# PEER gates added to a cleared table by 512 indirect transfers, expert rows added in memory, and expert blocks reordered

## Chip, cores and metric

The kernel runs on one core of a Trainium2 chip. The time is the device time of one execution in microseconds (us), the median of three runs.

## What is computed

Two transformer blocks on 512 tokens of width 1024, all in float32. The first has a spatial gating branch, a neighbourhood attention and a mixture of experts: 64 experts with 256 hidden units, of which each token takes 8. The second has a latent attention (MLA, 8 heads), a retention branch and a PEER layer with 16384 experts of one hidden unit each. The two parts that the change touches are, cut to what matters:

```
# experts (moe_ffn)
scores = sigmoid(h @ w_router); idx = top_k(scores + b_router, 8)
wts = scores[idx] / sum(scores[idx]) * 2.5
routed[tok] += swiglu(h[tok], w_gate[e], w_up[e], w_down[e]) * wt      # for each of a token's 8 experts
out = swiglu(h, w_sh_gate, w_sh_up, w_sh_down) + routed                # the shared expert
# PEER: 8 heads; a head's key scores against two sets of 128 keys
# 16 best of each set, 16 best of their 256 sums -> 16 of 16384 experts and softmax gates
y[tok] = sum over heads and their 16 experts of  gate * gelu(h[tok] . u[expert]) * v[expert]
```

## The kernel before

Each float32 operand of a large product is split into a high and a low half (`w_hi` by ScalarE, `w_lo` = raw - high by VectorE), and a product is three matmuls: high by high, high by low, low by high. Stages follow one another as blocks: when an `nc.Block()` ends, all engines wait for each other, which the trace shows as waits for `PEq`. `load` (L1125) is such a block: SP issues loads and waits for them.

**Experts (L1211).** Tokens stand in blocks of 128 rows: 4 blocks for the shared expert (`b < T`, T = 4), then 95: 64 for the experts' first 128 tokens each, 31 for what is over. Their order is two of the first kind, one of the second. Routing (VectorE, with small TensorE products) makes lists of rows for each block (`vtab`, and `tok` = `vtab` / 8). For a block GpSimd gathers the tokens' rows by an indirect transfer (`take`, L1355, four blocks ahead), gathers weights for the over blocks (L1366), and scatters the result (`put`, L1378) to `expert_rows`, which has one row for each of the 4096 pairs of token and slot. SP loads the weights of a base block, 3 MB in three units. TensorE goes `gate_up(b+1)` (24 matmuls), `turn_hidden(b)` (2 transposes), `turn_x(b+3)` (8), `down(b)` (12 matmuls). Between them ScalarE does SiLU and `hidden_high`, VectorE `multiply` and `hidden_low`; both also split the weights. After the last block follows the combine (L1736 to L1791): VectorE makes the slot weights, loads 8 rows and the shared row for each token, and adds them with one multiply-add for each slot.

**MLA attention (L539, called at L1934).** `attend` begins with `load` of a table `spread` of 0.2 KB and then goes through 32 units of 128 queries and a head.

**PEER (L2147).** 64 activation steps `n`, each with two groups of 128 experts: SP loads 1 MB of `peer_u` (two buffers), ScalarE and VectorE split it, TensorE does 48 matmuls, ScalarE applies GELU, SP stores the activations to `acts`. Then 64 value steps, each with 1 MB of `peer_v`, activations and gates fetched back and multiplied, and 48 matmuls. The routing rides on the first steps: in steps 0 to 15 two key products each and VectorE's 16-best searches (`key_round`), in steps 16 to 23 `pick` finds expert numbers, `divide` the softmax. In steps 25 to 57 the gates are put into place by one-hot products: for 4 tokens at a time (128 batches) VectorE makes `hot1` and `hot2`, TensorE multiplies them (`place`, L2523), ScalarE copies the result (`gate_copy`, L2319), and SP stores it to `gates` in 8 pieces of 4 MB. `fetch(0)` and `fetch(1)` (L2261, L2262) follow in step 62.

## Time and profile before

| what | us |
|---|---|
| median of 3 runs (4597.18 to 4601.25) | 4598.52 |
| profiled execution | 4600.06 |
| its span, first to last instruction | 4598.2 |
| TensorE matmul busy (85%) | 3897.8 |
| VectorE busy (54%) | 2492.4 |
| ScalarE busy (37%) | 1722.5 |
| GpSimd busy (10%) | 437.9 |
| mean granted TensorE clock | 0.906 of full |

PE is TensorE, PEld its weight loads, DVE VectorE, ACT ScalarE, POOL GpSimd, SP the queue that issues most transfers. Times inside the trace count from the first instruction. Shares are averages over stages that have different limits, so the stages are read one by one.

### The profile page before, as it was taken

To read this page: it belongs to the slowest core of one execution; us is meant where nothing else is said; L and a number is where in the kernel's file an instruction comes from. 1 tells how busy PE (TensorE), PEld (TensorE's weight loads), DVE (VectorE), ACT (ScalarE), POOL (GpSimd) and SP (SyncE) were. 2 spreads that over 40 slices of the span, in tenths; PEclk is the share of its full clock that TensorE was granted. 3 is DMA by queue.
4 is the path that set the end of the run, shared out by engine and by line. 5 is a ranking of instruction groups with operands and counts; after the bars stand their busy time and mean duration, and the time that the engine had idled before them with its cause. 6 is when DMAs were issued, how large, how long until landed. Compare 5 with 4: busy or idle time off the path is not lost. (4 is left out here: it accounts for less than half of the span.)

```text
span 4598.2 us, 46686 instructions
## 1 busy us (share of the span) xinstructions
PE 3897.8 (85%) x18351; PEld 3144.6 (68%) x18351; DVE 2492.4 (54%) x3841; ACT 1722.5 (37%) x2079; POOL 437.9 (10%) x295
## 2 busy tenths in 40 slices
PE   8677889669999999944399559789999999999999
PEld 1565767557777777733366447678888887888887
DVE  0334513458888888865643433359956663444444
ACT  0222512227777777732122023223233332222222
POOL 0001000014444444410000000000000000000000
PEclk9785879879999999976659779899999999999999
DMA  7210112326666666661002012224445555555554
GB/s 248 80 72 1 38 48 78 145 90 239 245 245 231 228 247 230 233 237 62 21 3 74 9 60 92 73 79 138 138 154 181 181 182 187 198 187 201 186 198 174
DMA packets 250053, 656.69 MB, mean 143 GB/s; under 512 B 44951, under 2 KB 144027, under 8 KB 206316
## 3 DMA queue, kind: packets, MB, share of 16 engines
q1 hardware_dynamic: 208508, 614.78, 37.9%
q0 software_dynamic: 41328, 38.93, 2.5%
q8 instruction: 147, 2.41, 0.2%
q14 instruction: 70, 0.57, 0.0%
HBM read 688.66 MB, written 125.31 MB: 177 GB/s over the span
## 5 line engine op out<-in xcount | busy, mean ns | idle before, releaser
L1503 DVE TENSOR_TENSOR w_lo<-w_raw,w_hi 128x2048 fp32r<-128x2048 f32 x288 | 651.6, 2290 | 172.4 <-ACT w_hi L1413 171.2
L1413 ACT ACTIVATE w_hi<-w_raw 128x2048 fp32r<-128x2048 f32 x288 | 539.3, 1907 | 7.2 <-DMA w_raw<-in_e_w,over_rows 4.3
L2362 DVE TENSOR_TENSOR w_lo<-w_raw,w_hi 128x2048 fp32r<-128x2048 f32 x128 | 293.2, 2290 | 351.1 <-ACT w_hi L2299 350.5
L2299 ACT ACTIVATE w_hi<-w_raw 128x2048 fp32r<-128x2048 f32 x128 | 245.3, 1916 | 523.0 <-DMA w_raw<-in_peer_u 274.9
L1144 PE MATMUL ps_peer<-peer_xT_hi,w_hi 128*128 128x512 f32 x1024 | 408.7, 399 | 4.1 <-DVE w_lo L2362 4.0
L1144 PE MATMUL ps_peer<-w_hi,coef_hi 128*128 128x512 f32 x1024 | 399.6, 390 | 6.1 <-DVE coef_lo L2459 6.1
L1146 PE MATMUL ps_peer<-peer_xT_hi,w_lo 128*128 128x512 f32 x1024 | 399.8, 390 | 0.0
L1145 PE MATMUL ps_peer<-peer_xT_lo,w_hi 128*128 128x512 f32 x1024 | 399.7, 390 | 0.0
L1145 PE MATMUL ps_peer<-w_lo,coef_hi 128*128 128x512 f32 x1024 | 399.3, 390 | 0.0
L1146 PE MATMUL ps_peer<-w_hi,coef_lo 128*128 128x512 f32 x1024 | 399.2, 390 | 0.0
L1626 PE MATMUL ps_gu<-w_hi,h2T_hi 128*128 128x512 f32 x792 | 311.0, 393 | 0.7 <-DVE w_lo L1503 0.7
L1628 PE MATMUL ps_gu<-w_hi,h2T_lo 128*128 128x512 f32 x792 | 310.7, 392 | 0.0
L1627 PE MATMUL ps_gu<-w_lo,h2T_hi 128*128 128x512 f32 x792 | 310.1, 391 | 0.0
L479 DVE TENSOR_TENSOR w_lo<-w,w_hi 128x1024 fp32r<-128x1024 f32 (+5 forms) x116 | 170.0, 1473 | 257.8 <-ACT w_hi L465 257.4
L465 ACT ACTIVATE w_hi<-w 128x1024 fp32r<-128x1024 f32 (+5 forms) x116 | 145.0, 1257 | 352.7 <-DMA w<-in_w_in 231.5
L1626 PE MATMUL ps_d<-w_hi,hidden_hi 128*128 128x512 f32 x396 | 169.3, 428 | 89.7 <-DVE hidden_lo L1515 89.7
L1144 PEld LDWEIGHTS ps_peer<-w_hi,coef_hi 128*128 128x128 f32 x1024 | 192.8, 188 | 47.2 <-issue 7.0
L1144 PEld LDWEIGHTS ps_peer<-peer_xT_hi,w_hi 128*128 128x128 f32 x1024 | 193.3, 189 | 43.4 <-DVE w_lo L2362 5.6
L1146 PEld LDWEIGHTS ps_peer<-peer_xT_hi,w_lo 128*128 128x128 f32 x1024 | 192.7, 188 | 40.7
L1146 PEld LDWEIGHTS ps_peer<-w_hi,coef_lo 128*128 128x128 f32 x1024 | 192.8, 188 | 40.2
L1145 PEld LDWEIGHTS ps_peer<-w_lo,coef_hi 128*128 128x128 f32 x1024 | 192.8, 188 | 39.8
L1145 PEld LDWEIGHTS ps_peer<-peer_xT_lo,w_hi 128*128 128x128 f32 x1024 | 193.1, 189 | 37.9
(475 smaller groups left out, 7584.6 us busy)
## 6 DMA issues: line engine op xcount, KB each, us to landing
w_raw<-in_e_w SPq DMA_DIRECT2D x195, 1024.0 KB, 4.8
w_raw<-in_peer_u SPq DMA_DIRECT2D x64, 1024.0 KB, 5.9
w_raw<-in_peer_v SPq DMA_DIRECT2D x64, 1024.0 KB, 4.8
acts<-act_out SPq DMA_DIRECT2D x64, 512.0 KB, 6.6
gates<-gate_tile SPq DMA_DIRECT2D x8, 4096.0 KB, 15.3
act_back<-acts SPq DMA_DIRECT2D x64, 512.0 KB, 5.8
gates_back<-gates SPq DMA_DIRECT2D x64, 512.0 KB, 7.0
w<-in_w_in SPq DMA_DIRECT2D x26, 1024.0 KB, 7.4
```

Source lines behind the costliest of these rows:

```text
L465: nc.scalar.activation(half_of(w_hi, b, half), half_of(w, b, half), ACT.Copy).then_inc(w_hi_done.sem, 1)
L479: nc.vector.tensor_tensor(half_of(w_lo, b, half), half_of(w, b, half), half_of(w_hi, b, half).bitcast(F32), ALU.subtract) \
L1144: nc.tensor.matmul(out, w_hi, x_hi, start=first, stop=False)
L1145: nc.tensor.matmul(out, w_hi, x_lo, start=False, stop=False)
L1146: return nc.tensor.matmul(out, w_lo, x_hi, start=False, stop=last)
L1413: nc.scalar.activation(w_hi[:, slot(n), :], w_raw[:, slot(n), :], ACT.Copy).then_inc(hi_done.sem, 1)
L1503: nc.vector.tensor_tensor(w_lo[:, slot(n), :], w_raw[:, slot(n), :], w_hi[:, slot(n), :].bitcast(F32), ALU.subtract).then_inc(lo_done.sem, 1)
L1626: nc.tensor.matmul(out, s_hi, m_hi, start=first, stop=False)
L1627: nc.tensor.matmul(out, s_hi, m_lo, start=False, stop=False)
L1628: return nc.tensor.matmul(out, s_lo, m_hi, start=False, stop=last)
L2299: nc.scalar.activation(w_hi[:, n % 2, :], w[:, n % 2, :], ACT.Copy).then_inc(w_hi_done.sem, 1)
L2362: nc.vector.tensor_tensor(w_lo[:, n % 2, :], w[:, n % 2, :], w_hi[:, n % 2, :].bitcast(F32), ALU.subtract) \
```

## The change

Three things change.

1. *PEER gates.* The table `gates` is one column of 128 * 128 * 512 floats. It is cleared by 16 transfers of 2 MB from a zeroed tile, issued ahead of the MLA attention. The one-hot products, their copies and stores go. VectorE makes for each gate its place in the table, and GpSimd adds the gates by indirect transfers with an add, each for 128 tokens and one of 8 * 16 gates: 4 * 128 = 512 transfers. The routing is done for tokens 0 to 255 (8 key steps, 4 pick steps) and then for 256 to 511, so that the first can be added early.
2. *Expert rows.* `put` adds a block's rows to the token's row in memory (`expert_rows` has 512 rows, which the shared expert writes first), each after the landing of the one before. The slot weights are made in the routing, kept in memory, gathered for each block, and applied by ScalarE's copy of the result. The combine reads 4 tiles.
3. *Order in the expert blocks.* `turn_hidden(b)` goes ahead of `gate_up(b+1)`, `hidden_high` and `hidden_low` ahead of the weight halves.

The diff, cut:

```diff
 # experts
@@ sync
+            sp.wait_ge(route_dve.sem, step["wk"])
+            sp.dma_start(scratch["slot_weights"].rearrange("(t p k) o -> p t (k o)", p=P, k=TOPK), wk[:]) \
+                .then_inc(wk_kept.sem, 16)
@@ gpsimd, take(b)
+                nc.gpsimd.indirect_dma_start(
+                    out=wslot[:, r:r + 1], out_offset=None, in_=scratch["slot_weights"],
+                    in_offset=bass.IndirectOffsetOnAxis(ap=vtab[:, r:r + 1], axis=0), bounds_check=V_PAD - 1,
                     oob_is_err=False).then_inc(x_in[b % 4].sem, 16)
@@ gpsimd, put(b)
+                if b == T:
+                    pool.wait_ge(stored[0].sem, 32)
+                    pool.wait_ge(stored[1].sem, 32)
+                else:
+                    pool.wait_ge(stored[(b - 1) % NO].sem, 16 * ((b - 1) // NO + 1))
                 nc.gpsimd.indirect_dma_start(
-                    out=scratch["expert_rows"], out_offset=bass.IndirectOffsetOnAxis(ap=vtab[:, r:r + 1], axis=0),
-                    in_=ob[:, b % NO, :], in_offset=None, bounds_check=V_PAD - 1, oob_is_err=False) \
+                    out=scratch["expert_rows"], out_offset=bass.IndirectOffsetOnAxis(ap=tok[:, r:r + 1], axis=0),
+                    in_=ob[:, b % NO, :], in_offset=None, bounds_check=S - 1, oob_is_err=False, compute_op=ALU.add) \
                     .then_inc(stored[b % NO].sem, 16)
@@ scalar, out(b)
-                    nc.scalar.activation(ob[:, b % NO, h * S:(h + 1) * S], ps_d[:, h, :], ACT.Copy) \
+                    weight = 1.0 if b < T else wslot[:, at_row[b - T]:at_row[b - T] + 1]
+                    nc.scalar.activation(ob[:, b % NO, h * S:(h + 1) * S], ps_d[:, h, :], ACT.Copy, scale=weight) \
@@ scalar, loop over b (vector's loop alike: hidden_low(b) ahead of low(n))
+                hidden_high(b)
                 if b > T:
                     out(b - 1)
...
-                hidden_high(b)
@@ vector, after multiply(0)
+            link(nc.vector.tensor_tensor(sc[:], sc[:], mask[:], ALU.mult))
...
+                ins = nc.vector.tensor_reduce(wk[:, t, :], pick[:, 1], AX, ALU.add)
@@ tensor, loop over b
+                turn_hidden(b)
                 if b + 1 < NB:
                     gate_up(b + 1)
-                turn_hidden(b)
@@ combine
+            sp.dma_start(gate_row[:], scratch["gate_row"][0].partition_broadcast(P)).then_inc(rows_in.sem, 16)
+            for t in range(T):
+                sp.dma_start(rows[:, t, :], scratch["expert_rows"][t * P:(t + 1) * P, :]).then_inc(rows_in.sem, 16)
+            sp.dma_start(x[:], scratch["x_kept"].rearrange("(t p) d -> p t d", p=P)).then_inc(x_back.sem, 16)
...
+                link(nc.vector.tensor_tensor(rows[:, t, :], rows[:, t, :], gate_row[:], ALU.mult))
...
+                nc.vector.tensor_tensor(x[:, t, :], x[:, t, :], rows[:, t, :], ALU.add)
-                for k in range(TOPK):
-                    link(nc.vector.scalar_tensor_tensor(acc, rows[:, t % 2, k, :], wk[:, t, k:k + 1], acc, ALU.mult,
-                                                        ALU.add))
 # second_mixer, between load(causal) and attend
+    zero = core.sb("zero_gates", [P, ZERO // P])
+    zero_gates(core, zero, scratch["gates"])
+def zero_gates(core, zero, gates):
+    with nc.Block() as block:
+        def _(dve):
+            nc.vector.memset(zero[:], 0.0).then_inc(cleared.sem, 1)
+        def _(sp):
+            sp.wait_ge(cleared.sem, 1)
+            for i in range(P * PNK * S // ZERO):
+                sp.dma_start(gates[i * ZERO:(i + 1) * ZERO, :].rearrange("(p n) o -> p (n o)", p=P), zero[:]) \
+                    .then_inc(zeroed.sem, 16)
 # after attend, a block in which SP waits for gates_zeroed
 # peer
-KEY_STEPS = 16
-PICK_STEPS = 2 * T
+KEY_STEPS = PH
+PICK_STEPS = 4
+def route_step(n):
+    pair, at = divmod(n, ROUTE_STEPS)
...
+    return "pick", (2 * pair + t, j)
@@ gpsimd (new)
+            for pair in range(T // 2):
+                for h in range(PH):
+                    for t in (2 * pair, 2 * pair + 1):
+                        if h == 0:
+                            pool.wait_ge(chosen_done.sem, t + 1)
+                        else:
+                            pool.wait_ge(scattered[t].sem, 16 * PK * h)
+                        for k in range(PK):
+                            nc.gpsimd.indirect_dma_start(
+                                out=scratch["gates"],
+                                out_offset=bass.IndirectOffsetOnAxis(ap=where[:, t, h, k:k + 1], axis=0),
+                                in_=chosen[:, 2, t, h, k:k + 1], in_offset=None, bounds_check=P * PNK * S - 1,
+                                oob_is_err=False, compute_op=ALU.add).then_inc(scattered[t].sem, 16)
@@ sync, step NG - 2, ahead of fetch(0)
+                    for t in range(T):
+                        sp.wait_ge(scattered[t].sem, 16 * PH * PK)
@@ vector, divide(t)
+                link(nc.vector.scalar_tensor_tensor(wheref[:], chosen[:, 0, t], float(PNK), chosen[:, 1, t], ALU.mult,
+                                                    ALU.add))
+                nc.vector.tensor_scalar(where[:, t], wheref[:], float(S), at_token[:, t:t + 1], ALU.mult, ALU.add)
@@ vector, tensor, scalar: hots(b), place(b), gate_copy(b), the 12 transposes of chosen go
-                nc.vector.tensor_tensor(hot1[:, q], iota[:].unsqueeze(1).to_broadcast([P, GB, PNK]),
-                    last = nc.tensor.matmul(bank[:, i], hot1[:, q, i], hot2[:, q, i], start=True, stop=True)
```

## Rows read from the trace of the kernel before

**Rows 1.** Busy time by stretch of PEER steps: length, PE, PEld, DVE, ACT, POOL; clock, DMA share.

```profile
3060.00:3180.00 120.00, 120.00 (x530) 99.38 (x530) 115.92 (x513) 35.05 (x50) 0.00 (x0) 1.00 0.41 131
...
3894.00:4598.00 704.00, 699.11 (x3072) 578.12 (x3072) 300.38 (x199) 187.44 (x126) 0.00 (x0) 0.99 0.55 189
```

**Rows 2.** Waits in the expert blocks, 1040 to 2010 us (total, times, longest).

```profile
PE ps_d L1626 <- DVE hidden_lo L1515: 78.3, 94, 2.2
```

**Rows 3.** Timeline of TensorE in one expert block (start us, us).

```profile
1450.37 0.50 PE L1626 MATMUL ps_d<-w_hi,hidden_hi 128*128 128x512 f32 x1 [0.81 <-DVE hidden_lo L1515]
```

**Rows 4.** Timeline of VectorE in the same block.

```profile
1445.48 4.49 DVE L1503 TENSOR_TENSOR w_lo<-w_raw,w_hi 128x2048 fp32r<-128x2048 f32 x2 [1.10 <-ACT w_hi L1413]
```

**Rows 5.** Timeline of VectorE from the expert stage's end through the combine.

```profile
2016.55 0.43 DVE L1740 TENSOR_TENSOR router_scores<-router_scores,router_mask 128x256 f32<-128x256 f32 x1 [11.87 <-PEq L1335]
...
2027.27 0.69 DVE L1781 TENSOR_REDUCE slot_weights<-slot_pick 128x8 f32<-128x512 f32 x1
2041.90 10.53 DVE L1788 SCALAR_TENSOR_TENSOR token_rows<-token_rows,slot_weights 128x1024 f32<-128x1024 f32 x8 [13.95 <-DMA token_rows<-shared_rows]
...
2093.28 1.23 DVE L1791 TENSOR_TENSOR x<-x,token_rows 128x1024 f32<-128x1024 f32 x1
```

**Rows 6.** Timeline of VectorE in the routing of the experts.

```profile
938.98 0.41 DVE L1558 TENSOR_SCALAR route_g<-route_g 64x512 f32<-64x512 f32 x1
```

**Rows 7.** Timeline of SP's queue around the MLA attention.

```profile
2305.20 0.26 SPq L1133 DMA_DIRECT2D spread<-in_k_spread  x1
2435.32 2.26 SPq L420 DMA_DIRECT2D w<-in_w_in  x4
```

**Rows 8.** Timeline of ScalarE where the attention begins.

```profile
2306.82 1.28 ACT L695 ACT_TABLE_LOAD   x1 [4.98 <-PEq L1129]
```

**Rows 9.** DMA issues: count, size of one, median us from issue to landing.

```profile
gates<-gate_tile SPq DMA_DIRECT2D x8, 4096.0 KB, 15.3
...
token_rows<-shared_rows SPq DMA_DIRECT2D x4, 512.0 KB, 16.6
...
out<-x SPq DMA_DIRECT2D x4, 512.0 KB, 2.6
...
x<-h_rows,slot_token POOLq DMA_INDIRECT x95, 4.2
```

**Rows 10.** Timeline of GpSimd where the expert blocks begin.

```profile
1003.29 1.87 POOL L1355 DMA_INDIRECT x<-h_rows,slot_token  x1 [0.30 <-issue]
1005.47 1.90 POOL L1355 DMA_INDIRECT x<-h_rows,slot_token  x1 [0.30 <-issue]
...
1025.30 0.99 POOL L1355 DMA_INDIRECT x<-h_rows,slot_token  x1 [0.30 <-issue]
```

**Rows 11.** Timeline of VectorE at the same place.

```profile
997.61 11.09 DVE L1503 TENSOR_TENSOR w_lo<-w_raw,w_hi 128x2048 fp32r<-128x2048 f32 x5
```

**Rows 12.** Groups of TensorE's matmuls in the PEER stage.

```profile
L1144 PE MATMUL ps_peer<-w_hi,coef_hi 128*128 128x512 f32 x1024 | 399.6, 390 | 6.1 <-DVE coef_lo L2459 6.1
...
L2523 PE MATMUL ps_peer<-hot_e,hot_e 128*128 128x128 f32 x1024 | 124.5, 275 | 0.0
```

**Rows 13.** The chain that ended last: PEER steps (start, us, what).

```profile
3067.70 0.86 PE ps_peer L2504 x4
...
3197.43 0.86 PE ps_peer L2504 x4
...
3335.72 0.50 PE ps_peer L1144
...
3364.62 1.78 PE ps_peer L2523 x16
...
3881.17 9.43 DMA gates_back<-gates
...
3895.36 0.77 PE ps_peer L1144
```

**Rows 14.** The queue of GpSimd's transfers: packets, MB, share of 16 engines' span.

```profile
q0 software_dynamic: 41328, 38.93, 2.5%
```

More of the change, by code:

```diff
@@ L1919, in second_mixer, with _ @@
     core.drop(qT, kT, kmT, kv, causal)
+    with nc.Block() as block:
+        @block.sync
+        def _(sp):
+            sp.wait_ge(core.sig("gates_zeroed").sem, 16 * (P * PNK * S // ZERO))
+    core.drop(zero)
     at = QL + KVL + MROPE
@@ L2225, in peer @@
         "coef_done", "coef_hi_done", "coef_lo_done", "y_mm", "added"))
-    acts_kept, gates_kept, acts_in, gates_in = ([core.sig(f"peer_{n}_even"), core.sig(f"peer_{n}_odd")] for n in (
-        "acts_kept", "gates_kept", "acts_back", "gates_back"))
-    out_done = core.sig("stored")
-    acts, gates = scratch["acts"], scratch["gates"]
-    def batches(step, part):
-        first = PER_STEP * (step - 1 - GATES_FROM) + part * PER_STEP // 2
-        return [b for b in range(first, first + PER_STEP // 2) if 0 <= b < NBATCH]
+    acts_kept, acts_in, gates_in = ([core.sig(f"peer_{n}_even"), core.sig(f"peer_{n}_odd")] for n in (
+        "acts_kept", "acts_back", "gates_back"))
+    out_done, zeroed = core.sig("stored"), core.sig("gates_zeroed")
+    acts, gates = scratch["acts"], scratch["gates"].rearrange("(p e t) o -> p e (t o)", p=P, e=PNK)
     with core.psum("ps_peer", [P, 8, S], F32) as ps, nc.Block() as block:
@@ L2274, in _ @@
                 sp.dma_start(acts[:, GE * n:GE * (n + 1), :], act_out[:, n % 2]).then_inc(acts_kept[n % 2].sem, 16)
[L2275 to L2279 removed]
                 if n == NG - 2:
+                    for t in range(T):
+                        sp.wait_ge(scattered[t].sem, 16 * PH * PK)
                     for q in range(2):
[L2282 removed]
                         sp.wait_ge(acts_kept[q].sem, 16 * (NG // 2 - 1))
```

297 lines of the change are left out of this document (115 added, 182 removed).

## Prediction

> **What bounds the kernel now.** I read the granted clock and the windows by stage first. TensorE is busy for all of a window of the PEER activation steps and for 699 of 704 us of the value steps, at full clock; the 16 DMA engines are 41 and 55% busy there [rows 1]. So the PEER stage goes by matmuls, while GpSimd is empty there. Then the waits of the expert stage: TensorE stands still ahead of `down` in nearly every block, 78.3 us over 94 blocks, until VectorE has written `hidden_lo` [rows 2], and the first matmul after such a wait lasts 0.50 us [rows 3] where a matmul's mean is 0.39 (399.6 us for 1024) [rows 12]. Last the short stages without matmuls: the combine (VectorE alone, 2016.55 to 2094.5) [rows 5] and the MLA attention, where the reader should look at the small load in front [rows 7, 8].
>
> **The expert blocks.** `turn_hidden(b)` moves ahead of `gate_up(b+1)`, and `hidden_high` and `hidden_low` move ahead of the weight halves. The 24 matmuls of `gate_up` (at the steps' pace, below, 5.5 us) then hide the copy and subtraction. What is late next is `multiply`: it needs SiLU after `gate_up`, and VectorE meanwhile does two weight halves, 4.49 us [rows 4]. Those start when ScalarE has its first half; I get `multiply` done about 8.7 us into a block of 9.4 us, so it is just in time, because `turn_x` and `down` (3.8 us) lie between. I take back 78 us and half of the slow first matmuls: -84. Bounds: 0, if VectorE becomes the bound, and -90.
>
> The slot weights move from the combine into the routing. Their work lasts from 2016.55 to 2027.96 with a gap of 0.55 [rows 5], so 10.9 us, and now stands between `multiply(0)` and the flags, where VectorE's chain goes on directly at 938.98 [rows 6] and TensorE waits for it: +11 (not under 7, since an idle gap of a few us lies later). Each `take` gets a second gather (95 in all), each `put` waits for the landing of the one before. GpSimd then issues four indirect transfers in a block instead of three, at 1.3 to 2.2 us each (below), at most 9 of 9.4 us, and the gathers run four blocks ahead: nothing. The scatter has one block to land; a gather of 128 rows lands in 4.2 us [rows 9], and an accumulation must read its rows too: twice that, 8.4, still fits: nothing, except at the end of the stage, where the last two follow at 4.5 us: +5. The bound is a stretch of the stage if the landing passes 9.4 us.
>
> The combine lasted 78.0 us (2016.55 to 2094.5): weights, 32 multiply-adds, 18 MB of loads [rows 5]. Now five issues (2.5 us), a landing of some 9.5 us for 2.5 MB (between 2.6 us for 0.5 MB and 15.3 us for 4 MB [rows 9]), four multiplications and four additions of 1.22 us (9.9 us). That is 22 us: -56. Experts together: -84 + 11 + 5 - 56 = -124.
>
> **Clearing the table.** 33.6 MB of zeros are written by 16 transfers ahead of the MLA attention, which looks like cover enough: it runs from 2306.82 to 2435.3, 128 us [rows 7, 8]. But `attend` begins with `load` of `spread`, at 2305.20, on the same SP queue, and waits for it. A load behind others on this queue lands after them: `token_rows<-shared_rows`, 0.5 MB, takes 16.6 us behind 4 MB, where `out<-x` of the same size lands in 2.6 us [rows 9]. So `spread` (0.2 KB) waits for nearly all zeros, and the cover is gone. Writing: 4 MB took 15.3 us [rows 9], less 2.6 of fixed time gives 12.7, eight times is 102, plus 2.6: 104 us. With the memset (4096 elements a partition, twice the 2048 that take 2.3 us at most: 4 us) and a block boundary of 1 us, against the 1.6 us that the load took: +107. Bounds: +6 if the small load overtakes (the zeros then just fit under the attention), +128 at 15.3 us for each 4 MB. VectorE and SP are stopped by the boundary, all engines wait.
>
> **PEER, TensorE.** The 1024 one-hot passes go [rows 12]; in the chain they stood as 64 pieces of 1.78 us, 113.9 us, and 12 transposes of 1.3 us. A step without them is 704/64 = 10.9 us or, with two key products, 11.79 us (from 3067.70 to 3197.43 in eleven steps [rows 13]). The order keys, picks, keys, picks has the same 24 steps, which ended at 3335.72 [rows 13]; then 40 steps of 10.92 us end the activations at 3772.5 where the kernel before came to 3889. VectorE's 230 us of one-hot work and ScalarE's gate copies go as well and were under TensorE.
>
> **PEER, GpSimd.** This takes its place. 512 indirect transfers go out one after the other, and `fetch(0)` waits for all. The price of one from the expert stage: free of VectorE 0.99 us with 0.30 us between, so 1.29 us [rows 10]; but while VectorE runs the back-to-back `w_lo` subtractions (11.09 us for five [rows 11]), the transfers end at one each 2.2 us, each 0.9 us after such a subtraction ends [rows 10]. So one `w_lo` of 2.29 us a step blocks the transfer that starts in it, for 0.9 to 2.2 us, mean 1.55: (10.92 - 1.55)/1.29 = 7.3 transfers a step, 1.50 us each. The price of a 4-byte row with an add is not in the trace. Transfers of 4 KB and of 8 KB rows both last 0.99 when free, so I take the same.
>
> Tokens 0 and 1 are ready by step 12, at 3197 [rows 13], with 16 transfers out before. Until 3336 come 139/1.50 = 93, until 3772.5 another 291: 400. The last 112 find VectorE idle: 144 us, to 3917, plus a landing of 4.2 [rows 9], 3921. From the fetch of the gates to the first value matmul it was 14.2 us (3881.17 to 3895.36) [rows 13]: values start at 3935 against 3895.4, +40 instead of the -117 of the matmuls. The groups of the same tokens wait for each other, but 16 others (21 us) lie between, against a landing of some 4 to 8 us: nothing. Values stay as they are (-0).
>
> **Sum.** -124 + 107 + 40 = +23. The profiled execution took 4600.1 us (span 4598.2), 1.5 above the median of 4598.5, so 4622 in the median's terms.
>
> **Rivals.**
> *The scatters are paced by more than GpSimd.* For: the software queue's packets take 2.5% of 16 engines over the span, 1839 us for 41328, 44.5 ns each [rows 14]; 8 rows and a semaphore per engine and scatter are 0.40 us, read twice 0.80, which is 62% of 1.29 us, and the weights already take 41% [rows 1]: full. Also an add may cost GpSimd more descriptors. Against: those packets are mostly of about 1 KB, these of 4 B. If a transfer costs 1.7 us, 496 of them end at 4040: +123, 4745; at 2.2 us, the slowest pace seen [rows 10], at 4288: +371, 4993. More is possible if each waits for the one before.
> The Trainium skill (DMA: Bandwidth & Descriptors, Anatomy of one DMA) gives every transfer from GpSimd a fixed cost of about 2 us, mostly the receipt, and its rules say to coalesce small ones. By that price, exposed each time, 496 transfers would be an estimated 992 us, about 4890. The trace speaks against exposure, since gathers that land in 4.2 us are issued each 1.29 us.
> *The small load isn't held up* (for: it uses few engines and bytes; against: [rows 9]). The clearing costs 6 instead of 107: 4521, faster than before. It decides early: with the clearing at +84 instead of +107 the change would cost nothing, below that it wins.
> *VectorE doesn't hold up 4-byte scatters.* Then 496 x 1.29 = 640 us, end 3837, -80: 4542, faster.
> *The accumulating `put` lands later than a block.* At 12 us for two blocks in three the stage loses about 3 us a block: with the gain of the reorder gone, 4780. I hold it in the first rival's upper part.
>
> **Chances and range.** My sum 0.42 (own range 4580 to 4680); paced by more, by scatters or by `put`, 0.32; load not held up 0.14; VectorE harmless 0.10; else 0.02. The first and second are slower but for the sum's lower edge. About 0.2% is what a measurement of this kernel tells from nothing: 4589 to 4608. Faster 0.26, same 0.06, slower 0.68. Range for 8 in 10: 4515 takes in both faster cases; up to 4890 half of the paced cases.
>
> **What the profile would show.** Blocks of 9.5 us instead of 10.4, no wait of `ps_d` for `hidden_lo`; from 938 to 998 eleven us more; combine 22 us. Between `causal` and the first attention matmul some 110 us with DMA engines full: if it is 5, the second rival is right. PEER steps of 10.9 us after the picks; GpSimd transfers at about 1.5 us, 1.29 at the end; TensorE idle some 150 us ahead of the values, waiting for `gates_back`. Wrong would be: a pitch far from 1.5, steps stretched beyond 10.9 by late weights (then the scatters' packets crowd them), or blocks that wait for `stored`.

## The result: 6.6% slower, outside the predicted range

Time after: 4918.4 us median of 4 runs (4913.8 to 4918.6), against 4599.9 us for the kernel before on the same chip; the ratio is 1.066, 95% interval 1.058 to 1.074. One of the four times of the kernel before is 4654.2 where the others are 4597.2 to 4601.3, and it pulls this ratio down; by the medians it is 1.069. The prediction was 4622 us, range 4515 to 4890. The sign was right, the size was not: +318.6 us between the two profiled spans (4598.2 and 4916.8) where +23 was forecast.

The page of the changed kernel first: busy time of each engine, then the span in 40 slices (123 us each).

```profile
span 4916.8 us, 45029 instructions
...
PE   7759888679999999333966887999995000899999
...
POOL 0010000056767765000000000388888888000000
PEclk9886979789999999665888898999997555999999
DMA  6210022257777877206101222466664222555544
GB/s 237 83 53 1 35 79 86 108 186 247 255 253 244 257 250 223 69 22 273 52 25 39 77 77 89 131 129 148 149 142 77 0 0 0 191 187 188 185 188 171
```

Slices 32 to 34 are the picture of this case: PE shows 0, POOL shows 8, and 0 GB/s are moved. Nothing but GpSimd works there, and not on anything large. A second hole, shorter, is in slices 18 and 19, with 273 GB/s: the zeros.

The windows give the four stretches that matter (length; busy time and instructions of PE, PEld, DVE, ACT, POOL; granted clock; DMA share; GB/s).

```profile
2207.30:2295.00 87.70, 0.00 (x0) 0.00 (x0) 3.47 (x1) 0.00 (x0) 0.00 (x0) 0.52 0.91 386
3200.00:3700.00 500.00, 495.70 (x2174) 408.49 (x2173) 191.08 (x390) 143.44 (x149) 425.30 (x232) 1.00 0.63 142
3770.00:4180.00 410.00, 0.00 (x0) 0.00 (x0) 0.00 (x0) 0.00 (x0) 342.92 (x221) 0.50 0.24 0
4190.00:4900.00 710.00, 706.49 (x3019) 567.48 (x3020) 296.24 (x191) 189.19 (x129) 0.00 (x0) 0.99 0.50 186
```

The first is the clearing, the second the activation steps, the third the hole, the fourth the value steps. In the one-hot steps of the kernel before (3400 to 3880) VectorE was busy for 266 us of 480; in these it is 191 of 500, and TensorE is as full as before (495.7 of 500, and 478.9 of 480). In the hole it has the clock at 0.50, the lower level, and no instruction. TensorE's waits in 3700 to 4300 (us in total, times, longest):

```profile
PE ps_peer L1144 <- DVE coef_lo L2471: 439.5, 1, 439.5
```

And SyncE's own in the same stretch:

```profile
SPq L2300 <- DMA gates<-chosen,gate_at: 439.8, 1, 439.8
```

SyncE's fetch of the gates waits once, 439.8 us, for the landing of the last transfer into `gates`, and TensorE's first value matmul once, 439.5 us, for `coef_lo`, which follows the fetch. The chain of waits goes through the same place:

```profile
4180.54 2.88 DMA gates<-chosen,gate_at
4184.02 4.30 DMA gates_back<-gates
```

The last transfer starts at 4180.5, and 12.5 us later the first value matmul starts (the way over the landing, the fetch, VectorE's product and the two halves). Now the instructions of the tile `gates` (shortest, median, longest duration in ns; first and last start):

```profile
L2325 POOL DMA_INDIRECT gates<-chosen,gate_at x512: 1552/1553/3395, 3147.9 to 4180.5; - x171
...
DMA to landing us min/median/max: 2.9/3.2/49.5
```

This is the line on which the prediction fails. A transfer of 128 rows of four bytes with an add takes GpSimd 1552 ns at the least and 1553 in the median, and 0.30 us lie between two: one each 1.86 us with VectorE idle. I had taken 0.99 + 0.30 = 1.29 us.

**Where the 318.6 us are.** I cut both spans at two loads that both kernels make, that of `causal` ahead of the MLA attention (2302.3 before, 2207.3 after) and that of `iota` at the start of PEER (3048.5 and 3024.6).

| stretch | before | after | difference | predicted |
|---|---|---|---|---|
| to `causal` (routing, expert blocks, combine) | 2302.3 | 2207.3 | -95.0 | -124 |
| `causal` to `iota` (clearing, attention, mixer) | 746.2 | 817.3 | +71.1 | +107 |
| `iota` to the end (PEER) | 1549.7 | 1892.2 | +342.5 | +40 |

PEER by its own parts: the first value matmul starts at 4193.0 after 439.5 us of waiting, so the activations end at 3753.5. They take 728.9 us from `iota` against 840.5 (-112, predicted -117); the wait is 439.5 us against 6.4 (+433, predicted +156); and the value stage takes 723.8 us against the 702.8 from 3895.4 [rows 13] to the end (+21, predicted nothing).

### The profile page after: what moved, and what is told of

The parts are those of the page before. It is cut to its first block and busy times, and to the rows that moved or that the text cites. A ratio compares the mean times of both kernels' runs of the same rounds, so it can differ in the third digit from the quotient of the medians.

```text
span 4916.8 us, 45029 instructions
## 1 busy us (share of the span) xinstructions
PE 3784.1 (77%) x17315; PEld 3020.0 (61%) x17315; DVE 2234.5 (45%) x3185; ACT 1672.0 (34%) x1954; POOL 1551.9 (32%) x902
## 5 line engine op out<-in xcount | busy, mean ns | idle before, releaser
L2325 POOL DMA_INDIRECT gates<-chosen,gate_at x512 | 874.2, 1708 | 1336.3 <-DVE chosen L2460 1176.3
L1144 PE MATMUL ps_peer<-w_hi,coef_hi 128*128 128x512 f32 x1024 | 405.3, 396 | 440.0 <-DVE coef_lo L2471 439.5
L1660 PE MATMUL ps_gu<-w_hi,h2T_hi 128*128 128x512 f32 x792 | 322.6, 407 | 0.7 <-DVE w_lo L1520 0.7
L2355 ACT ACTIVATE coef_hi<-act_back 128x1024 fp32r<-128x1024 f32 x64 | 67.9, 1060 | 717.5 <-DVE act_back L2467 452.5
L2467 DVE TENSOR_TENSOR act_back<-act_back,gates_back 128x1024 f32<-128x1024 f32 x64 | 78.0, 1218 | 446.7 <-DMA gates_back<-gates 446.7
L1393 POOL DMA_INDIRECT expert_rows<-block_out,slot_token x95 | 208.1, 2191 | 132.3 <-ACT block_out L1449 59.7
```

Of the source, the lines that this page charges most:

```text
L1144: nc.tensor.matmul(out, w_hi, x_hi, start=first, stop=False)
L1393: nc.gpsimd.indirect_dma_start(out=scratch["expert_rows"], out_offset=bass.IndirectOffsetOnAxis(ap=tok[:, r:r + 1], axis=0), in_=ob[:, b % ...
L1660: nc.tensor.matmul(out, s_hi, m_hi, start=first, stop=False)
L2325: nc.gpsimd.indirect_dma_start(out=scratch["gates"], out_offset=bass.IndirectOffsetOnAxis(ap=where[:, t, h, k:k + 1], axis=0), in_=chosen[ ...
```

## Experiments

Each run was timed in three rounds beside the kernel before on its own chip. Chips differ by some 15 us in 4600, so runs on different chips are compared by their ratio to the kernel before or by stretches of the trace.

**1. The transfers write instead of adding.**

```diff
 in_=chosen[:, 2, t, h, k:k + 1], in_offset=None, bounds_check=P * PNK * S - 1,
-oob_is_err=False, compute_op=ALU.add).then_inc(scattered[t].sem, 16)
+oob_is_err=False).then_inc(scattered[t].sem, 16)
```

> Edit: the 512 transfers of the gates write their rows instead of adding them; the rest, their order and their waits too, is as in the changed kernel. Where two heads of a token chose the same place, one gate takes the place of the sum, so this leaves out that addition. Theory A (the add itself costs GpSimd the 0.56 us by which one transfer, 1.55 us, is longer than the 0.99 us row of the plain store): transfers fall to about 0.99 us plus 0.30 us, the wait of TensorE for the gates falls from 424 us to about 145 us, and the time is 4620 to 4670 us. Rival B (the 1.55 us belongs to rows of four bytes in a table of 8.4 million rows, whatever is done to them): the operation stays at 1.55 us and the time at 4918 us. Rival C (the transfers are paced by the landing in memory and GpSimd's time only shows it): an add reads and writes, so part of it goes; 4700 to 4850 us with operations whose length varies.

Measured: 4652.9 us (4649.7 to 4661.9), ratio 1.013 (1.010 to 1.016). The same line of the trace:

```profile
L2325 POOL DMA_INDIRECT gates<-chosen,gate_at x512: 982/984/3051, 3143.4 to 3917.9; - x171
```

And GpSimd's instructions in order of time (start, duration, idle before), first of the changed kernel:

```profile
3560.64 1.55 POOL L2325 DMA_INDIRECT gates<-chosen,gate_at  x1 [0.31 <-issue]
3562.50 1.55 POOL L2325 DMA_INDIRECT gates<-chosen,gate_at  x1 [0.30 <-issue]
3564.36 1.55 POOL L2325 DMA_INDIRECT gates<-chosen,gate_at  x1 [0.30 <-issue]
3566.22 3.07 POOL L2325 DMA_INDIRECT gates<-chosen,gate_at  x1 [0.30 <-issue]
3569.59 1.55 POOL L2325 DMA_INDIRECT gates<-chosen,gate_at  x1 [0.30 <-issue]
3571.45 1.55 POOL L2325 DMA_INDIRECT gates<-chosen,gate_at  x1 [0.30 <-issue]
```

Then of this run:

```profile
3564.62 0.98 POOL L2325 DMA_INDIRECT gates<-chosen,gate_at  x1 [0.30 <-issue]
3565.91 0.98 POOL L2325 DMA_INDIRECT gates<-chosen,gate_at  x1 [0.30 <-issue]
3567.20 0.98 POOL L2325 DMA_INDIRECT gates<-chosen,gate_at  x1 [0.31 <-issue]
3568.49 2.86 POOL L2325 DMA_INDIRECT gates<-chosen,gate_at  x1 [0.30 <-issue]
3571.66 0.98 POOL L2325 DMA_INDIRECT gates<-chosen,gate_at  x1 [0.31 <-issue]
3572.95 0.98 POOL L2325 DMA_INDIRECT gates<-chosen,gate_at  x1 [0.30 <-issue]
```

In both, most transfers have one exact length and one a step is longer. The long ones start during VectorE's `w_lo` (2.29 us from 3565.57 in the changed kernel, from 3568.20 in this run), and once the activations are over and VectorE is idle there is none: the longest of the changed kernel's last 231 is 1572 ns. Without the add the length is 0.98, with it 1.55. Theory A holds in the length, and 4653 lies in its window; TensorE's wait fell to 184.4 us and not to the 145 expected, since more transfers are left over at the end (see below). B is out by the 0.98, C by lengths that don't vary. The add's price doesn't depend on the size of a row either: `put` in the expert stage carries rows of 4 KB, and its shortest instruction is 973 ns without an add, in the kernel before:

```profile
L1378 POOL DMA_INDIRECT expert_rows<-block_out,slot_row x95: 973/1019/3141, 1037.5 to 2009.2; - x95
```

With an add, in the changed kernel, it is 1552 ns:

```profile
L1393 POOL DMA_INDIRECT expert_rows<-block_out,slot_token x95: 1552/1617/3707, 1052.0 to 1970.0; - x95
```

The software queue's row of the changed kernel's page (packets, MB, share of 16 engines) shows what is made in that time:

```profile
q0 software_dynamic: 118096, 39.31, 7.8%
```

In run 1 it is:

```profile
q0 software_dynamic: 60752, 39.31, 4.2%
```

57,344 packets more for 512 transfers: 112 each. The run with 256 transfers (next) has 81,232 packets, 36,864 fewer than the changed kernel, so one transfer of four-byte rows makes 144 packets with an add and 32 without. It would be tempting to put GpSimd's 0.57 us down to the additional packets, but the expert stage speaks against it. There the add changes GpSimd's shortest time in the same way, and the packets not at all. Run 3 below, whose `put` adds:

```profile
q0 software_dynamic: 44368, 39.01, 4.0%
```

Run 8, whose `put` writes (shortest 975 ns):

```profile
q0 software_dynamic: 44368, 38.98, 2.7%
```

All of these counts come out exactly with 144 packets for every transfer of 128 rows but one kind, the plain transfer of four-byte rows, which makes 32: the 41,328 of the kernel before [rows 14] are 287 times 144 (95 gathers, 95 puts, 93 weight loads, 4 direct), run 3 has 95 times 32 more for the fetches of weights, and run 1 and the changed kernel have 512 times 32 and 512 times 144 on top of that. A plain one of 4 KB rows then takes GpSimd 0.98 us for 144 packets, as one of four-byte rows does for 32. So the 0.57 us goes with the add and not with the number of packets; what GpSimd does in it no run here shows.

**2. Half the transfers.**

```diff
-                            pool.wait_ge(scattered[t].sem, 16 * PK * h)
-                        for k in range(PK):
+                            pool.wait_ge(scattered[t].sem, 8 * PK * h)
+                        for k in range(PK // 2):
```

> Edit: of each head only the first eight of sixteen gates are added, 256 transfers in all; this leaves out half the gates. Theory A and B alike (GpSimd's own 1.86 us for each transfer sets the end): the second half of the table is done before the activations end near 3762 us, TensorE's wait of 424 us falls to what the fetch of activations and gates needs, about 15 us, and the time is 4490 to 4520 us. Rival (something other than the number of transfers holds the values back, such as the clearing or a landing after the last one): the wait falls by less than half and the time stays over 4700 us.

Measured: 4477.8 us (4476.4 to 4490.0), ratio 0.975 (0.972 to 0.978), 12 us under the window.

The tile `gates` in it:

```profile
L2325 POOL DMA_INDIRECT gates<-chosen,gate_at x256: 1553/1553/3564, 3149.1 to 3702.9; - x128
```

The last transfer starts at 3702.9, ahead of the end of the activations, and TensorE's wait is gone. So the number of transfers times the time of each is all that held the values back; and even transfers that cost nothing on the path would leave the kernel only 2.5% better than before, with the clearing still in.

**3. and 4. The two halves of the change by themselves.** The kernel before with the expert stage of the changed one, and the changed kernel with the expert stage of before (whole functions exchanged, no lines of their own).

> Edit: the kernel before with the changed expert stage alone (new order in the blocks, weighted rows added in memory); gates made by one-hot products as before, no table cleared. Theory: the load behind the expert stage comes 95 us earlier in the changed kernel and nothing after it knows of that, so 4600 - 95 = 4505 us (4500 to 4512). Rival (part of the 95 us is owed to the other part, or is given back later): 4520 to 4560 us.

> Edit: the changed kernel with the expert stage of before; the table is cleared and filled by the 512 transfers. Theory: the parts are independent and add up: 4918 + 95 = 5013 us (5005 to 5020). Rival (the parts share something, such as the clearing running slower or faster by what stands before it): off that sum by more than 15 us.

Measured: experts only 4490.5 us (4480.0 to 4500.7), ratio 0.977 (0.973 to 0.980); gates only 5023.1 us (5004.2 to 5069.4), ratio 1.095 (1.087 to 1.102). The parts are -106 and +427 us against the kernel before beside them (4596.0), together +321, and the change as a whole is +318.6. Experts only lies 9.5 us under its narrow window. Gates only lies 3 us over its own and 10 over the 5013 of its theory; its rival began at 15. The parts add up, no shared cost shows beyond the spread of the runs (5004 to 5069 for gates only), and the expert stage is a gain that the rest buried.

**5. and 6. What the clearing costs.** In 5 the zeros are issued by SyncE inside attention's block, in 6 by the block of their own as before, but after the small load has landed.

```diff
     load(core, [(spread[:], core.spread[dv][0:G, 0:R])])
+    if then is not None:
+        then()
...
     load(core, [(causal[:], a["k_causal"])])
     zero = core.sb("zero_gates", [P, ZERO // P])
-    zero_gates(core, zero, scratch["gates"])
...
+           lambda: zero_gates(core, zero, scratch["gates"]))
```

That is run 6: `attend` calls what stands behind `lambda` as `then`. In run 5 the zeroed tile is set by GpSimd and SyncE's part stands within attention's block, as

```diff
+    @block.sync
+    def _(sp):
+        sp.wait_ge(cleared.sem, 1)
+        for i in range(P * PNK * S // ZERO):
+            sp.dma_start(gates[i * ZERO:(i + 1) * ZERO, :].rearrange("(p n) o -> p (n o)", p=P), zero[:]) \
+                .then_inc(zeroed.sem, 16)
```

> Edit: in the changed kernel the small load that attention waits for goes out first, and the 16 writes of zeros are issued by SyncE inside attention's own block, with the zeroed tile set by GpSimd there; nothing is left out. Theory (attention's start was held by the zeros in two ways: SyncE needed 37 us to issue them, and the small load then landed 38 us later behind them): the whole cost of 72 us goes, 4918 - 72 = 4846 us, at most 10 us more if the writes reach past attention into the next weight load. Rival (attention itself or what follows needs the memory that the zeros take, so the cost only moves): 4870 to 4918 us.

> Edit: in the changed kernel only the order of two steps is turned: the small load that attention waits for lands first, then comes the block that issues the 16 writes of zeros, then attention. Theory (two costs one after the other): the 38 us of waiting for the small load go, the 37 us in which SyncE issues stay, since attention's block starts when the block before it has ended: 4918 - 36 = 4882 us (4876 to 4888). Rival (the queue's order is all of it, and SyncE's issuing runs beside attention): 4846 us as in the run beside it.

Measured: 4836.2 us (4826.3 to 4853.9), ratio 1.056 (1.053 to 1.059), and 4885.9 us (4876.8 to 4896.8), ratio 1.067 (1.065 to 1.069). By medians the gains are 82 us (10 more than the theory of run 5) and 32 us (in the window of run 6), though the kernel before was 17 us faster on this chip; by the ratios of the medians they are 64 and 14 us. The stage marks decide it without that. From the load of `causal` to the first matmul of attention it is 4.6 us before, 88.0 us in the changed kernel, 46.3 us in run 6 and 4.8 us in run 5. SyncE's 16 issues in the changed kernel (shortest, median, longest ns; first and last start):

```profile
L1823 SPq DMA_DIRECT2D gates<-zero_gates x16: 326/1256/6707, 2214.8 to 2247.4; - x16
```

The issues of `spread`, the second of which is attention's:

```profile
L1133 SPq DMA_DIRECT2D spread<-in_k_spread x2: 252/2585/4918, 377.6 to 2252.0; - x2
```

And SyncE's wait for it:

```profile
SPq L1129 <- DMA spread<-in_k_spread: 37.9, 1, 37.9
```

SyncE is held for 37 us by the 16 issues (one of them for 6.7 us) and then waits 37.9 us for `spread`. Two costs one after the other, each of which one of the runs takes away.

Attention itself does not run alike in these kernels. The kernel before, 110 us from the first matmul (columns as in the windows above):

```profile
2306.86:2416.86 110.00, 109.03 (x405) 70.58 (x406) 46.13 (x202) 30.67 (x140) 0.00 (x0) 0.55 0.00 1
```

The same 110 us of the changed kernel:

```profile
2295.28:2405.28 110.00, 108.67 (x479) 71.39 (x479) 53.67 (x231) 35.76 (x157) 0.00 (x0) 0.67 0.00 1
```

And of run 5, where the zeros go out beside it:

```profile
2214.70:2324.70 110.00, 106.99 (x512) 70.56 (x512) 56.39 (x240) 37.23 (x161) 3.48 (x1) 0.74 0.73 306
```

At a granted clock of 0.55 attention takes 128.5 us up to the next weight load, at 0.67 it takes 117, at 0.74 it takes 110. Run 8 below has no zeros and stands at 0.72 with 112 us, and run 3, without zeros too, at 0.52 with 132 us, so it is not the zeros that raise it. What does is open. Runs 10 and 12 below are the same program up to this point and far beyond it, and stand at 0.55 (129 us) and 0.72 (112 us), so the program alone doesn't decide it: it can be the chip or the single execution, and only one execution of each was profiled. It is up to 20 us that no part of the change owns, and it makes 11 of the 12 us between the 83.4 us by which attention starts later and the +71.1 of the table.

**7. The new order alone.** The kernel before, in which only these lines change places (and ScalarE's `hidden_high(b)`, which likewise goes ahead of the weight halves).

```diff
             for b in range(T, NB):
+                turn_hidden(b)
                 if b + 1 < NB:
                     gate_up(b + 1)
-                turn_hidden(b)
...
+                hidden_low(b)
                 for n in ready:
                     if units[n][1] < 2:
                         low(n)
-                hidden_low(b)
```

> Edit: the kernel before with only the new order of instructions in the expert blocks (the hidden rows are turned ahead of the next gate and up products, and their two halves come ahead of the weights' halves); weights, stores and combining as before. Theory: each block loses the wait of about 0.9 us for the second half of the hidden rows and falls from 10.38 us to about 9.3 us, 84 to 100 us in all: 4500 to 4516 us. Rival (without the adding in memory GpSimd has less to do, so blocks get shorter still than in the changed kernel): under 4495 us, so that combining and weighting in memory were worth nothing or a loss.

**8. Rows written, not added** (experts only, one-hot gates): `compute_op=ALU.add` taken from the `put` of an expert block.

> Edit: expert stage changed alone (one-hot gates as before), and each block's 128 weighted rows are written and not added; this leaves out the sum over experts. Theory (the add costs GpSimd 0.58 us for each block and a read of every row, and delays the weight loads queued behind it): GpSimd's store falls from 2.1 to about 1.6 us, the 57 us of ScalarE's waits for weights shrink, and the time is 4490 - 10 to 20 = 4470 to 4480 us. Rival (blocks are bound by TensorE and the other engines, with GpSimd's share hidden): 4490 us within 5.

**9. No fetch of slot weights** (experts only): the second transfer of `take` is gone, and `turn_x` waits for 16 in place of 32.

> Edit: expert stage changed alone (one-hot gates as before), without GpSimd's 95 transfers that fetch a weight for each slot of a block; the scale is then read from a tile of zeros, so this leaves out the experts' weights. Blocks took 10.35 us in the kernel before, 9.38 with the new order alone, 9.69 with the whole changed stage and 9.56 with its rows written and not added. Theory (GpSimd's extra work, 0.6 us for the add and 1.6 us for the fetch of weights, holds back the weight loads in its queue): blocks of 9.45 to 9.55 us, 14 to 22 us less over 95 blocks than with the whole stage; ratio to the kernel before about 0.973. Rival (the 0.31 us over the new order alone comes from the memory traffic of the added rows and the fetch, of four bytes a row, costs nothing): 9.65 to 9.70 us.

Measured: 7: 4491.8 us (4481.4 to 4509.0), ratio 0.980 (0.977 to 0.982). 8: 4472.2 us (4461.0 to 4478.1), ratio 0.976 (0.975 to 0.978). 9: 4462.2 us (4457.3 to 4468.7), ratio 0.972 (0.969 to 0.974). Run 3 is at 0.977. The ratios are too close to each other; the blocks are not. `h2T_hi` is written once a block, so the last start less the first is 94 blocks. Experts only (run 3):

```profile
L1455 ACT ACTIVATE h2T_hi<-ps_x x95: 1015/1027/1043, 1017.9 to 1928.8; 128x1024 fp32r<-128x1024 f32 x95
```

The new order alone (7):

```profile
L1438 ACT ACTIVATE h2T_hi<-ps_x x95: 1023/1027/1054, 1009.3 to 1890.9; 128x1024 fp32r<-128x1024 f32 x95
```

Rows written (8):

```profile
L1455 ACT ACTIVATE h2T_hi<-ps_x x95: 1016/1030/1051, 1017.4 to 1916.3; 128x1024 fp32r<-128x1024 f32 x95
```

No fetch of weights (9):

```profile
L1451 ACT ACTIVATE h2T_hi<-ps_x x95: 1016/1029/1057, 1026.2 to 1916.9; 128x1024 fp32r<-128x1024 f32 x95
```

That is 910.9, 881.6, 898.9 and 890.7 us, or 9.69, 9.38, 9.56 and 9.48 us a block, against 973.3 us and 10.35 before. The new order is worth 92 us. What was added with it takes 29 us back; taken away one at a time, the add gives 12 us and the fetch of weights 20. These small figures want care: nine profiled kernels here (the changed one and runs 1, 2, 3, 5, 6, 10, 11, 12) have the same expert stage, and their 94 blocks take 907.0 to 925.3 us. Run 8 lies 8 us under the lowest of them and run 9 16 us, so both are likely gains, but neither is measured to 10 us.

The block of run 7 takes 9.38 us, close to the 9.3 of its theory. Its rival expected blocks still shorter than in the changed kernel, which holds too (9.38 against 9.78), and from that a total under 4495 (it is 4492), so that weighting and combining in memory would be worth nothing or a loss. That last step doesn't follow. The ratios, 0.977 for run 3 and 0.980 for run 7, don't separate the two (their intervals overlap), but in the traces run 3 reaches the load of `causal` at 2196.6 and run 7 at 2213.3: it loses 29 us in the blocks and 9 ahead of them and gains 55 in the combine. In 8 the theory of the add fits by the 12 us in the blocks, within the care above, while the ratios don't tell it from its rival. In 9 the blocks of 9.48 us lie in the theory's window. The waits of ScalarE for weights in some 890 us of blocks show the way it takes (us in total, times, longest). Experts only:

```profile
ACT w_hi L1429 <- DMA w_raw<-in_e_w,over_rows: 56.7, 34, 3.8
```

Without the fetch of weights (9):

```profile
ACT w_hi L1425 <- DMA w_raw<-in_e_w,over_rows: 36.8, 37, 3.9
```

In run 8 they are 43.3 us. The new order alone (7):

```profile
ACT w_hi L1413 <- DMA w_raw<-in_e_w,over_rows: 9.4, 7, 4.2
```

The weight loads of the over blocks are issued by GpSimd, in the same queue as the adds and the fetches, so what holds GpSimd up delays them, and ScalarE, VectorE and TensorE wait in turn. For the fetch of weights it is GpSimd's time: from 1050 to 1940 GpSimd is busy for 616 of 890 us in run 3 and for 504 in run 9, while the DMA share doesn't fall (0.77 and 0.79). For the add that doesn't hold: in run 8 GpSimd is busy for 632 us, more than in run 3, and the blocks are shorter all the same. What falls there is its waits for the landing of the `put` before (37.4 us to 6.5) and the DMA share (0.77 to 0.72). Which of these gives the 12 us was not separated.

**10. Half and half.** Gates of the first 256 tokens by 256 transfers into a half table cleared beside attention, those of the last 256 by one-hot products from step 25 on. The core of it:

```diff
+PER_STEP = 2
...
+GATES_FROM = 2 * ROUTE_STEPS + 1
...
-            for pair in range(T // 2):
+            for pair in range(1):
...
                 activations(n, 0)
+                for b in batches(n, 0):
+                    place(b)
                 activations(n, 1)
+                for b in batches(n, 1):
+                    place(b)
```

> Edit: the changed kernel with zeros written beside attention, half a table cleared, the gates of the first 256 tokens added by 256 transfers and those of the last 256 made by one-hot products, two groups of four tokens a step from step 25 on; the table is laid out in eight chunks of tokens as before; nothing is left out. Theory: 256 transfers at 1.9 to 2.1 us from the twelfth step on are done some 100 us ahead of the activations' end, so they are hidden; the activations take 711 us plus half of the 130 us that the products cost, 776 us against 841 of the one-hot kernel; with the expert stage of 4490 us that gives 4425 us (4410 to 4440), the first version in which the transfers gain. Rival (VectorE's one-hot rows hold GpSimd's transfers back as its weight halves do, by 1.5 us each): the transfers end after the activations and the time is over 4450 us.

Measured: 4448.6 us (4446.0 to 4464.8), ratio 0.969 (0.966 to 0.971), 9 us over the window. The theory's mechanism holds: the last transfer starts at 3624.0, ahead of the end of the activations, whose results are written from 2959.8 to 3737.8, 778 us (776 forecast), against 830 us in experts only. But from `iota` to the end it is 1517.3 us against 1547.3, so of these 52 us only 30 arrive. 21 are lost in the value stage, which is what the window missed and what led to the last two runs. One of its three matmul lines in 550 us, experts only (count, busy us, mean ns):

```profile
L1145 PE MATMUL ps_peer<-w_lo,coef_hi 128*128 128x512 f32 x810 | 315.2, 389 | 0.0
```

The changed kernel:

```profile
L1145 PE MATMUL ps_peer<-w_lo,coef_hi 128*128 128x512 f32 x785 | 310.0, 395 | 0.0
```

Half and half:

```profile
L1148 PE MATMUL ps_peer<-w_lo,coef_hi 128*128 128x512 f32 x785 | 310.5, 396 | 0.0
```

The clock is 1.00 in all, but of all three lines together 2428 matmuls are recorded in the first and 2356 in the second: 0.227 us from one to the next against 0.233.

**11. and 12. The tiles of the value stage moved**, in the changed kernel and in half and half.

```diff
+    pad = core.sb("pad", [P, 14272 // 4])
     av, gv = core.sb("act_back", [P, 2, GE, S]), core.sb("gates_back", [P, 2, GE, S])
     c_hi, c_lo = core.sb("coef_hi", [P, 2, GE, S], F32R), core.sb("coef_lo", [P, 2, GE, S], F32R)
```

> Edit: in the changed kernel 14,272 bytes are left free in each partition ahead of the four tiles that the value stage works in (activations, gates and the two halves of the coefficients), so that they lie where the kernel before has them, at 131,008 in place of 116,736; nothing else changes. In the value stage a matmul of 512 columns follows the last one after 0.227 us in the kernels with one-hot gates and after 0.233 us in all kernels with the transfers, at a granted clock of 1.00 in both: 20 us over the 3072 of them. Theory (it is the place of the tiles in SBUF): the pace returns to 0.227 us and the time falls from 4918 to about 4898 us. Rival (it hangs on something else that the transfers bring, their table in memory or GpSimd): the pace stays at 0.233 us and the time at 4918 us.

> Edit: the kernel with half the gates by transfers and half by one-hot products, with 3,008 bytes left free ahead of the same four tiles, which then begin at 139,200, the place of the kernel before plus 8,192. Theory (place in SBUF, as in the run beside it): pace 0.227 us, 4448 - 20 = 4428 us. Rival: 0.233 us and 4448 us.

Measured: 11: 4908.5 us (4893.8 to 4916.8), ratio 1.069 (1.065 to 1.073). 12: 4431.0 us (4423.8 to 4447.1), ratio 0.966 (0.963 to 0.970).

The windows of 550 us again, run 11:

```profile
4260.00:4810.00 550.00, 549.59 (x2425) 454.70 (x2424) 234.31 (x152) 149.92 (x101) 0.00 (x0) 1.00 0.52 193
```

Run 12:

```profile
3800.00:4350.00 550.00, 550.00 (x2429) 455.40 (x2428) 234.57 (x152) 150.79 (x101) 0.00 (x0) 1.00 0.57 195
```

2425 and 2429 matmuls in 550 us: the pace is back in both. It is the place in SBUF: in run 11 the value stage takes 703.7 us (4204.3 to 4908.0) instead of 723.8. The time of 11 alone would not show it (4898 was forecast): 10 us less by the median, and nothing by the ratio, since its load of `iota` comes 7.5 us later, at 3032.1. Run 12 is the fastest version here and beats both kernels, the one before by 3.4%. Against run 10 it gains 18 us by the medians, near the 20 forecast, and 10 by the ratios, whose intervals overlap. The value stage alone went from 723.3 to 703.0 us; the profiled spans differ by 41, since attention too ran faster in the execution of run 12.

## Why the prediction was wrong

**The step that failed: the price of one transfer.** "The price of a 4-byte row with an add is not in the trace. Transfers of 4 KB and of 8 KB rows both last 0.99 when free, so I take the same." The part on size was right: plain rows of four bytes take 0.98 (run 1). The part on the add was not: 1.55. Everything after it was right in kind. At the forecast price, in run 1, 134 transfers are left when the activations end (from 3745.2 to 3917.9 at 1.29), where I had 112. At the real price 230 are left (3753.5 to 4180.5 at 1.86). So 427 us of transfers stand behind the activations in place of 144, and the wait is +433 in place of +156: 277 of the 295 us by which the sum was off. Run 1 parts these 277. With the price as forecast the wait is 184.4 us, +178, so 255 us come from the price and 22 from what VectorE holds up, which was put a little too low (below). That the rest of the sum was only 18 us off is in part luck: clearing came out 36 us cheaper than forecast, experts 29, values 21 and activations 5 us dearer.

A row that could have warned is not in the trace of before, since no transfer there adds, and the prediction looked at the wrong object for its bound. It looked for the add's cost in the DMA engines, where it found a share of 62%, and named GpSimd's descriptors in half a sentence ("an add may cost GpSimd more descriptors"). GpSimd's own time was it, though not by more descriptors: a transfer of 4 KB rows makes 144 packets with or without the add (runs 3 and 8). Its count of 8 rows and a semaphore on 16 engines, 144, is what an adding transfer makes, and its 0.40 us nearly what it costs the DMA engines (24% of 1.86 us alone with the transfers, 0.45 us; 2% in run 1); the doubling to 0.80 is not in the trace. Its own line between 1.7 us (4745) and 2.2 us (4993) gives 4824 at 1.86. That line takes the price as the pace of all transfers, and with the ones that VectorE holds up the pace was 2.02 us (512 from 3147.9 to 4180.5), at which it gives 4904, close to the 4918 measured. 4824 lies inside the stated range, which ended at 4890, and 4904 just outside.

**VectorE holds up a transfer a step.** Right. One transfer each step lasts 3.1 us in place of 1.55. I had 1.50 us each against 1.29 free, 0.21 more; the 46 to 49 transfers in each 100 us of the steps are 2.04 to 2.17 us each against 1.86, 0.2 to 0.3 more, and in run 1 it is 0.2 to 0.4 (60 to 66, 1.52 to 1.67 against 1.29). That is where the 22 transfers more in run 1 come from.

**Rival: paced by more than GpSimd.** Its number was nearer, its main reason wrong (above). **Rival: the accumulating `put` lands later than a block.** Mostly not: it lands in 7.7 us (median), and GpSimd waits for it 22 times, 37.4 us in all, 2.7 at most. But the forecast had "nothing" there, and these waits stand ahead of weight loads; they are part of what the blocks lost (run 8 drops them). The rival's own sum doesn't come out as written: 2.6 us over the block in two of three are 160 us, as its 4780 has, and not "about 3 us a block". **Rival: VectorE harmless.** Wrong, as said.

**The Trainium skill** (DMA: Bandwidth & Descriptors, Anatomy of one DMA) gives about 2 us for every transfer from GpSimd, mostly its receipt, and the estimate from it was 4890. As a number it came near by luck: the transfers land 2.9 us after their issue and are issued each 1.86, so the receipt overlaps; what doesn't is GpSimd's own time, which with VectorE's hold-ups happens to average 2.02 us. Its rule to coalesce small transfers (same page, Rules for kernel authors) no run here tries, since none joins any; run 2 shows only that half as many end the hole.

**Clearing: +107 predicted, +71 measured.** The mechanism was right: `spread` lands last, and attention, long enough as cover, starts after it (runs 5 and 6). The zeros went faster than by the row of 15.3 us for 4 MB: 33.6 MB from 2214.85 to 2294.9, 80 us in place of 104, at 419 GB/s. Attention starts 83 us later; 11 us came back by its higher clock.

**Experts: -124 predicted, -95 measured.** The blocks as a whole give -54 (973.3 and 919.1 us) in place of -84. Order of the blocks -84 predicted, -92 alone (run 7). Combine with the last puts -51 predicted (-56 and +5), -56 measured (from the last `h2T_hi` to `causal`, 322.8 and 267.1 us). Routing +11 predicted, +15 measured (first `h2T_hi` of the blocks at 1006.2 and 1021.1), of which 3 stand ahead of the changed part (`h2T_hi<-h2T` begins at 909.7 and 912.9), so +12. "Nothing" for the additional transfers was the wrong term: the blocks of the changed kernel take 9.78 us, 919.1 for 94, 37.5 us more than the order alone allows. GpSimd was counted at 9 of 9.4 us a block and called harmless because all of it fits; it is busy for some 70% of the time (616 of 890 us in run 3), waits in between for landings and results, and what stands behind it in the queue goes out late. Of TensorE's waits only this one is left in the window 1050 to 1940 of run 3, where [rows 2] had the one for `hidden_lo`:

```profile
PE ps_h L1685 <- DVE hidden L1527: 29.2, 19, 2.7
```

The wait for `hidden_lo` is gone and `turn_hidden` waits for `hidden` in its place, as said under "what is late next".

**Values: nothing predicted, +21 measured.** The place of four tiles (runs 11 and 12). The 440 idle us ahead, with the clock at 0.50, cost the value stage almost nothing here: with the tiles moved the stage takes 703.7 us behind such a wait against 702.8 in the kernel before.

**Sums.** A step without the products is 704/64 = 11.0 us and not 10.9; over 40 steps that is 3 us. VectorE's one-hot work is 263 us (512 of 0.34 and 128 of 0.69), not 230, and no term of the sum uses it. The activations, forecast to end 724 us after `iota`, took 728.9.

## What to carry to other kernels

A transfer with an add costs GpSimd a price of its own: take it from a row that adds, and if none exists give it a rival and let the range reach that. Count everything in GpSimd's queue, its waits too, since a queue that was busy for 70% of the time here delayed the loads behind it even though each single item seemed to fit. A small load that somebody waits for goes out ahead of large writes, and large writes are issued inside the block that covers them. When a stage of pure matmuls changes its pace without a reason in the program, look at where its tiles lie.

## What was not expected of the hardware

- An indirect transfer of 128 rows takes GpSimd 0.98 us, with rows of 4 bytes, 4 KB or 8 KB alike; with an add 1.55 us, with rows of 4 bytes and of 4 KB; 0.30 us between two. It makes 144 packets, with an add or without, but for the plain one of four-byte rows, which makes 32; GpSimd's time doesn't follow the packets.
- An indirect transfer that starts during VectorE's `w_lo`, which reads two tiles in SBUF for 2.29 us, lasts longer: 2.86 us in place of 0.98 and 3.07 in place of 1.55 in the rows above, at most 3.05 in run 1 and 3.40 in the changed kernel.
- Matmuls with the same operands and clock follow each other at 0.227 or 0.233 us, by where the tiles of the stage lie: slower with `act_back` at 116,736 and at 136,192, faster at 131,008 and 139,200. (The places are those that the program gives the tiles.) What in the address decides is open; nothing finer was tried.
- Attention ran at a granted clock of 0.52 to 0.55 or 0.65 to 0.74 in kernels whose code for it is the same, 128 to 132 us against 110 to 120.
- SyncE is held for 37 us while it issues 16 writes of 2 MB, up to 6.7 us for one.
